# MLP weights of a Griffin and differential-attention trunk: one more product's weights read through the ring, one quarter sum and the norm's sums of squares made by accumulating DMAs

## The reference

```
def rmsnorm(x, g, eps=NORM_EPS):
    x32 = x.astype(jnp.float32)
    y = x32 * lax.rsqrt(jnp.mean(x32 * x32, axis=-1, keepdims=True) + eps)
    return (y * g.astype(jnp.float32)).astype(x.dtype)

def sq_relu_mlp(h, w1, w2):
    u = jax.nn.relu(h @ w1)
    return (u * u) @ w2
...
    for l in range(DEPTH):
        if l < N_A_LAYERS:
            x = x + recurrent_block(rmsnorm(x, a_norm[l]), ...)
        else:
            x = x + diff_attention(rmsnorm(x, b_norm[j]), ...)
        x = x + sq_relu_mlp(rmsnorm(x, mlp_norm[l]), mlp_w1[l], mlp_w2[l])
```

## Time and profile before

| what | value |
| --- | --- |
| median of 3 runs | 1112.58 us (1108.49 to 1112.94) |
| the profiled execution, own time | 1110.49 us |
| its span, first to last instruction | 1108.4 us |
| TensorE / VectorE / ScalarE / GpSimd busy | 94% / 74% / 59% / 11% |
| mean granted TensorE clock | 0.984 |
| moved by SyncE's queue / by GpSimd's accumulating DMAs | 101.2 MB / 50.3 MB |

### The profile page before, as it was taken

How to read it: one execution, slowest core, us unless ns; L and a number is a source line. 1 busy time by engine, 2 the same in 40 slices (tenths; PEclk the granted TensorE clock), 3 DMA queues, 4 the chain that set the end, 5 groups by cost and what they waited for, 6 DMA issues and landing times.

```text
span 1108.4 us, 15255 instructions
## 1 busy us (share of the span) xinstructions
PE 1045.5 (94%) x5904; PEld 889.5 (80%) x5904; DVE 818.6 (74%) x1157; ACT 649.8 (59%) x940; POOL 122.8 (11%) x137
## 2 busy tenths in 40 slices
PE   8999988999999999999999999978999999999996
PEld 6778878889878879878877777757978978978975
DVE  7889766777776786798656666467687687687687
ACT  6689655645635745755336565556663664663665
POOL 1000041121101101100000000023011011011012
PEclk9999998999999999999999999998999999999998
DMA  7222257596596496562321211163576776776772
GB/s 254 76 76 95 79 150 168 118 246 169 120 241 150 122 240 167 125 168 80 114 76 39 73 42 42 55 190 60 170 174 159 200 170 161 202 167 158 207 141 107
DMA packets 43559, 153.75 MB, mean 139 GB/s; under 512 B 4960, under 2 KB 5088, under 8 KB 43360
## 3 DMA queue, kind: packets, MB, share of 16 engines
q1 hardware_dynamic: 29232, 101.20, 27.6%
q0 software_dynamic: 13824, 50.34, 24.8%
q10 hardware_dynamic: 432, 1.24, 0.3%
HBM read 150.66 MB, written 2.10 MB: 138 GB/s over the span
## 4 chain that ended last, share of the span: by engine, by line
PE 54%; DVE 19%; DMA 9%; ACT 8%; issue 8%; POOL 1%; SPq 0%; ACTq 0%; DVEq 0%; POOLq 0%
PE ps L1939 20%; PE ps L1811 19%; DMA q<-weights 9%; DVE w_lo L1111 8%; PE ps L2037 4%; PE ps L1974 3%; ACT w_hi L618 3%; DVE value L1477 3%; PE ps L2096 2%; DVE a_lo L1466 2%; DVE r L1439 2%; PE ps L2122 2%; ACT r L865 2%; PE ps L1865 1%; PE ps L2111 1%
## 5 line engine op out<-in xcount | busy, mean ns | idle before, releaser
L1939 PE MATMUL ps<-x_hi,w_hi 128*128 128x256 f32 x896 | 258.9, 289 | 23.2 <-DVE w_lo L1111 21.4
L1111 DVE TENSOR_TENSOR w_lo<-q,w_hi 128x1024 fp32r<-128x1024 f32 x160 | 197.4, 1240 | 111.1 <-ACT w_hi L618 110.8
L618 ACT ACTIVATE w_hi<-q 128x1024 fp32r<-128x1024 f32 x160 | 167.3, 1053 | 176.8 <-DMA q<-weights 73.4
L1939 PE MATMUL ps<-x_lo,w_hi 128*128 128x256 f32 x896 | 257.0, 287 | 0.0
L1939 PE MATMUL ps<-x_hi,w_lo 128*128 128x256 f32 x896 | 257.0, 287 | 0.0
L1939 PEld LDWEIGHTS ps<-x_hi,w_hi 128*128 128x128 f32 x896 | 175.5, 196 | 26.9 <-issue 13.9
L1974 PE MATMUL ps<-w_hi,a_hi 128*128 128x512 f32 x448 | 176.6, 394 | 17.3 <-issue 9.5
L547 POOL DMA_DIRECT2D q<-weights x96 | 82.5, 941 | 921.7 <-DMA q<-weights 458.6
L1111 DVE TENSOR_TENSOR w_lo<-w_raw,w_hi 128x1024 fp32r<-128x1024 f32 x118 | 143.8, 1220 | 44.6 <-ACT w_hi L618 44.3
L1939 PEld LDWEIGHTS ps<-x_lo,w_hi 128*128 128x128 f32 x896 | 175.7, 196 | 0.1
L1939 PEld LDWEIGHTS ps<-x_hi,w_lo 128*128 128x128 f32 x896 | 175.5, 196 | 0.0
(11 more groups left out here) (214 smaller groups left out, 1670.0 us busy)
## 6 DMA issues: line engine op xcount, KB each, us to landing
w_raw<-weights SPq DMA_DIRECT2D x118, 512.0 KB, 3.8
q<-weights POOLq DMA_DIRECT2D x96, 512.0 KB, 8.2
q<-weights SPq DMA_DIRECT2D x64, 512.0 KB, 4.6
x<-x_t SPq DMA_DIRECT2D x8, 256.0 KB, 5.8
y_t<-value SPq DMA_DIRECT2D x8, 256.0 KB, 2.3
w_raw<-weights SPq DMA_DIRECT2D x4, 256.0 KB, 4.9
gw<-gate_weights ACTq DMA_DIRECT2D x1, 1024.0 KB, 6.2
gain_rows<-final_gain SPq DMA_DIRECT2D x1, 512.0 KB, 6.3
```

The costliest lines, as they stand in the source:

```text
L618: nc.scalar.activation(w_hi[:, t % RING, :], src, ACT.Copy).then_inc(whi_done, 1)
L1111: nc.vector.tensor_tensor(w_lo[:, t % RING, :], src, w_hi[:, t % RING, :], ALU.subtract).then_inc(wlo_done, 1)
L1939: ins = nc.tensor.matmul(to, w[:, t % RING, ws], o[:, op, j, :], start=fresh and j == 0 and f % 2 == 0 and n == 0, stop=j == PAIRS - 1 and ...
```

## The change

`SOURCES` now reads A11 (tiles 0 and 1) and B11 (tiles 14 and 15) from the ring. In each group this adds four loads to the ring (`R_PER` 8 to 12). `q1` now gets A21 as its load at the group's start, and A11 by an accumulating DMA, for tiles 8 and 9. VectorE's `quarter_sum` remains for tiles 4 and 5 only and adds A11 from `w_raw`, which holds A11 until then; the ring's load of A12 waits for that add. The other sum, B11+B12, is now an accumulating DMA into `q1` (`SUMS` of `q1` 3 to 4), and the one of B22 into `q2` is issued before that of B22 into `q1`. GpSimd no longer adds squares: ScalarE writes the first two into `acc` and `rstd`, and six accumulating DMAs from `work` add the others, three to each; `stats` runs eight matmuls instead of four. In `residual_step` both engines split a weight tile before the rest of their chunk's work, and the high parts and rests of a pair's sums are taken one chunk later. In `mlp`, `act_sum` 1 and `act_hi` 1 come before the splitting of what they stood behind, and `act_hi` 2 and 3, `act_lo` 2 and `act_sum` 3 one or two steps earlier.

```diff
-SOURCES = (("q1", 0, 0, 0), ("q2", 0, 1, 0), ("q2", 0, 1, 1), None, ("q1", 0, 1, 0), ("q2", 0, 2, 0), None,
-           ("q1", 1, 1, 0), ("q1", 1, 1, 2), ("q1", 1, 2, 0), None, ("q2", 1, 3, 0), None, ("q1", 1, 3, 0))
-SUMS = {"q1": 3, "q2": 3}
+SOURCES = (None, ("q2", 0, 1, 0), ("q2", 0, 1, 1), None, ("q1", 0, 1, 0), ("q2", 0, 2, 0), None,
+           None, ("q1", 1, 2, 0), ("q1", 1, 3, 0), None, ("q2", 1, 3, 0), None, ("q1", 1, 4, 0))
+SUMS = {"q1": 4, "q2": 3}
...
-R_PER = 8
+R_PER = 12
...
                 load_quarter(layer, g, "q2", A21, down_tile(layer, g - 1, 8) if g else None)
                 if g:
-                    two(r, A12)
-                    load_quarter(layer, g, "q1", A11, down_tile(layer, g - 1, 12))
+                    two(r, A11)
+                    load_quarter(layer, g, "q1", A21, down_tile(layer, g - 1, 12))
...
-                two(r + 2, A22)
+                for half in range(2):
+
+                    sp.wait_ge(quarter_added, quarter_adds(layer, g, half))
+                    load_ring(r + 2 + half, stored_tile(layer, g, A12 + half))
+                two(r + 4, A22)
                 load_quarter(layer, g, "q1", B11, up_tile(layer, g, 8))
                 load_quarter(layer, g, "q2", B12, up_tile(layer, g, 10))
-                two(r + 4, B22)
-                two(r + 6, B21)
+                two(r + 6, B11)
+                two(r + 8, B22)
+                two(r + 10, B21)
...
             def add_others(layer, g):
-                add_quarter(layer, g, "q1", A21, split=up_tile(layer, g, 0), added=0)
+                add_quarter(layer, g, "q1", A11, loaded=0)
                 add_quarter(layer, g, "q2", A12, split=up_tile(layer, g, 4))
+                add_quarter(layer, g, "q1", B12, loaded=1)
+                add_quarter(layer, g, "q2", B22, loaded=1)
                 add_quarter(layer, g, "q1", B22, split=down_tile(layer, g, 2))
-                add_quarter(layer, g, "q2", B22, loaded=1, added=1)
                 add_quarter(layer, g, "q1", B21, split=down_tile(layer, g, 4))
...
+                for m in range(2, NCH):
                     pool.wait_ge(sq_done, n * NCH + m + 1)
-                    if k:
-                        pool.wait_ge(acc_done, k)
...
+                    if m > 3 or layer:
+                        pool.wait_ge(squares_in[m % 2], 16 * ((PAIRS - 1) * layer + m // 2 - 1))
+                    nc.gpsimd.dma_start((acc, rstd)[m % 2][:, :], work[:, m % 4, :],
+                                        accum_op=ALU.add).then_inc(squares_in[m % 2], 16)
...
                 for m in range(NCH):
                     j = m // 2
+                    if m < NCH - 1:
+                        split_hi(t + m + RING)
                     act.wait_ge(bank_read, b + m + 1)
...
+                    if m == NCH - 1:
+                        sums_hi(j)
+                        split_hi(t + m + RING)
+                    square(layer, m)
...
-                    if s in (11, 12):
-                        quarter_sum(layer, g, 1, s - 11)
...
-                pe.wait_ge(acc_done, n * NCH)
+                sums = (acc,) if n == N_KV else (acc, rstd)
...
+                else:
+                    for chain in squares_in:
+                        pe.wait_ge(chain, 16 * (PAIRS - 1) * (1 if n == N_M0 else 2))
```

119 lines of the change are left out of this document (60 added, 59 removed).

## The result

| | before | after |
|---|---|---|
| median of the runs | 1111.39 us | 1097.11 us (1093.88 to 1098.95, 4 runs) |
| profiled execution | 1110.5 us | 1095.56 us |
| its span | 1108.4 us | 1093.7 us |
| mean granted clock | 0.984 | 0.992 |
| TensorE idle before up products | 23.2 us | 2.4 us |

The ratio is 0.9871, with an interval of 0.9836 to 0.9907: faster by 1.3%, some 14 us. The forecast was 1068 us with a range from 1053 to 1090, so the direction came and a third of the size, and the time lies 7 us outside the range.

What follows compares the result with a forecast made beforehand. TensorE, busy 94% of the span, was taken to lose time only to stops at three places and a lower clock. From 1110.5 us, -23.6 - 15.9 - 4 gave 1067, said as 1068 for the median, range 1053 to 1090.

Steps and rivals of the forecast that it cites:

- A: Residual step before each MLP: TensorE's stops and the lower clock behind them go, -23.6 us in all.
- R3: Rival, residual steps: the squares' transfers land after 9 us or more and `stats` stops TensorE; 1080 us, chance 10%.
- B: Starts of groups 1 to 3 in each MLP: six stops and two falls of the clock go, -15.9 us.
- C: Turn from up to down products in eight groups: 0.5 us gained a group, -4 us, between -17.3 and +16.
- R2: Rival, the turn: B11's loads take 7.6 us or more, costing +16, and A11 lands late; 1088 us, chance 18%.
- R4: Rival, the turn: DMA engines bound it, B11 lands after 10 us, A11 misses, clock falls; 1134 us, chance 7%.

Runs made afterwards that it cites:

- the kernel with both parts: The kernel before with the squares added by accumulating DMAs and the new order of the residual step, nothing else: 1079.62 us, ratio 0.9731.
- the corners: Four kernels: the change 1097 us, without B12's accumulating DMAs 1091, with `q1`'s B22 ahead of `q2`'s 1081, with both edits 1061.

## Why the prediction was right in two parts and wrong in the third

**A, the residual steps: right.** Taken at -23.6, the stages gave -23.1. The wait of ScalarE for GpSimd went, and the clock stayed at 1.00 as forecast. Of the six transfers of squares in layer 0, which the forecast had bounded by 5.0 and 12.2 us, three landed in 3.3 us and the last in 5.2; the first two took 11.8 and 12.6, behind A22's sums in the queue. TensorE's one wait for them is 0.2 us, so R3 did not come. One stop of 1.8 us stayed in layer 1. Alone, A was worth more, -29; a part of that is clock elsewhere, since the kernel before has 0.83 over 10 us at two group starts and the kernel with both parts at one. That A's larger part can come from the order, not from the transfer that takes GpSimd's adds away, the forecast did not see. By the Trainium skill (SBUF — State Buffer, "SBUF: two separate sides") the descriptors of GpSimd's DMAs wait while VectorE runs an instruction in a two-port mode. 3.3 us to landing beside a VectorE that is busy for 66% of that stretch gives no sign of such a wait; no run here tells whether any of its instructions there were in that mode.

**B, the group starts: right**, -15.9 forecast, about -16 in the stages, -14 to -16 by itself. In group 2 the loads of the next group's A11, issued at 313.49 and 315.95 us, took 9.2 and 10.5 us, near the 9.7 of the earlier trace rows, and TensorE did not stop at the next group's start.

**C, the turn: wrong, and it is the whole error.** The step that failed is the sentence that takes the ring load of B11 at 5.5 us, and so -4 us. The loads took 7.65 and 8.32 us in the group shown and 7.8 us in the mean of all sixteen, past the upper bound of 7.6 that I had given the price, and cost 24.5 us, above the bound of +16. The price of 5.5 us was wrong as well: with the order of before the loads took 5.9 us in the mean, and TensorE's idle time before down products was still 5.8 us above that of the kernel before, where I had a gain of 4. Three things were missed, the first two readable before the run.

First, the order in GpSimd's queue. Part C says that the accumulating DMAs of B12 and B22 are in flight and prices no more of it. R2 discounts its own case by saying that there is now one at a time. But the change puts `q2`'s B22 ahead of `q1`'s, and takes from it the wait for VectorE's sum. What had been held back to after tile 17 now goes out exactly when B11 is loaded. And it was not one at a time: when the first of these loads was issued, at 271.88 us, both of B12's accumulating DMAs were in flight (265.03 us, landed after 8.7, and 267.43, after 10.2). Trading the two lines back gives 16 us.

Second, that transfers pass their delay to the next. `q2`'s loads of B12, issued beside B12's first accumulating DMA at 265.79 and 268.67 us, took 8.1 and 9.1 us; the second accumulating DMA then landed only at 277.6 us, and B11's loads ran beside it. The sum by VectorE in place of B12's accumulates gives another 12 us (1080.89 to 1068.55; 11 by the ratios). Alone each cure gives less than together, which the corners show.

Third, the clock. A stop before down product 2 was followed by 10 us at 0.83 three times, which no stop of place C had caused before. The forecast gave R4 this loss and left it out of R2, which else has the right mechanism and nearly the right price: a load at 7.6 us or more and +16 for the turn, 1088 us. The idle time added is 34.8 - 17.3 = 17.5 us, the clock some 1.7 us three times, 5.1, together 22.6 of the 24.5; the last 2 us I cannot assign. The rows of the kernel before show no such fall at the turn, and not all of it hangs on the late loads: the kernel with the sum by VectorE, whose loads are in time, also has 0.83 over 10 us twice (216 and 952.6 us), behind stops of 1.85 and 1.80 us before product 3.

With loads in time the forecast's working holds. The run with the sum by VectorE has the stop before product 1 gone and one left before product 3, 2.8 us less idle time before down products than the kernel before, at 1068.6 us. The rule on the queues that R2 names, the Trainium skill (DMA: Bandwidth & Descriptors, section on SWDGE, HWDGE and iDMA), by which a DMA engine serves its queues in turn, agrees in direction: 3.4 to 4.3 us without an accumulating DMA in flight, 4.4 to 10.2 us with one or more. My estimate for half of each engine is twice the 3.5 us, 7.0; the longer ones lost more than that, and no run here takes apart to what. The chance of 18% for R2 was the misjudged number, and the range left its worse half out: R2's sum is 1088.9, and with the 2 us from the profiled execution to the median, which the forecast added for itself and not for R2, it is 1091, beyond the upper end of 1090.

R4's mechanism (the burst of transfers) came in part, without its price: A11 did not miss, so B stayed.

## What to carry to other kernels

Before a vector sum is given to an accumulating DMA, look at which load with a short deadline is issued in the next 10 us, not at the mean share of the DMA engines: here a relief of 20 us of VectorE's time cost 12 us, and the place of one line in GpSimd's queue 16. When a change takes a wait from a queued transfer, ask what that wait had kept out of the way. And a chain of instructions on an engine should have the waiting for a load behind what others need, as the order of the residual step did: it gave 17 us with the wait left in, on the kernel before.
